# Head norms: each tile's sum of squares issued inside the next tile's products, and a gate chunk ahead of the first attention

## What is computed

```python
q = rmsnorm(q.reshape(bsz, s, B_HEADS, 2, B_HEAD_DIM), q_norm_g[l]).transpose(0, 2, 3, 1, 4)
k = rmsnorm(k.reshape(bsz, s, B_HEADS, 2, B_HEAD_DIM), k_norm_g[l]).transpose(0, 2, 3, 1, 4)
...
o = diff_attention(q, k, vb, lam, slopes)
...
gates = jax.nn.sigmoid(h @ w_gate[l] + b_gate[l])
```

## Time and profile before

| | |
|---|---|
| Median of 3 runs | 1939.25 us (1938.33 to 1940.53) |
| Profiled execution, its own time | 1938.46 us |
| Its span | 1936.5 us |
| Granted TensorE clock, mean | 0.965 |
| Busy: TensorE, its weight loads | 1814.7 us, 1333.3 us |
| Busy: VectorE, GpSimd, ScalarE | 898.5 us, 719.3 us, 590.1 us |

### The profile page before, as it was taken

One profiled execution on the slowest core, in us unless ns is written; L12 is line 12 of the kernel. 1 busy time (PEld: TensorE's weight loads), 2 busy tenths in 40 slices (PEclk: granted clock), 3 DMA queues, 4 the chain that ended last, 5 costly groups with the idle time before them and its releaser, 6 DMA issues.

```text
span 1936.5 us, 22752 instructions
## 1 busy us (share of the span) xinstructions
PE 1814.7 (94%) x8562; PEld 1333.3 (69%) x8562; DVE 898.5 (46%) x1267; ACT 590.1 (30%) x1085; POOL 719.3 (37%) x413
## 2 busy tenths in 40 slices
PE   5999979999998899999799889999989979999999
PEld 3888757775876444443488776777767868888887
DVE  4220665654453233332523576999438663303331
ACT  2323334444233111010232334555335222212221
POOL 4444323333340100000121447888814424444442
PEclk8999989999998899999889899999999989999999
DMA  5322222224343699999422332112253313332221
GB/s 198 98 77 98 78 75 66 82 82 141 95 133 120 237 396 394 343 365 375 170 77 86 132 97 92 68 66 71 77 195 108 121 56 108 98 98 90 96 97 44
DMA packets 81892, 266.32 MB, mean 138 GB/s; under 512 B 8320, under 2 KB 9344, under 8 KB 81792
## 3 DMA queue, kind: packets, MB, share of 16 engines
q1 hardware_dynamic: 60864, 222.32, 32.4%
q10 hardware_dynamic: 18624, 34.21, 5.0%
q0 software_dynamic: 2304, 8.39, 1.3%
HBM read 248.11 MB, written 16.78 MB: 137 GB/s over the span
## 4 chain that ended last, share of the span: by engine, by line
PE 86%; DVE 7%; DMA 3%; ACT 2%; issue 1%; ACTq 1%; POOL 0%; SPq 0%; DVEq 0%
PE psum L550 83%; DMA more<-stream 2%; DVE root L1769 1%; PE psum L1147 1%; DVE area_r L1743 1%; PE psum L846 1%; ACTq L1680 1%; PE psum L641 1%; DVE area L2273 1%; DVE root L1748 1%; ACT root L1290 1%; ACT area L1290 1%; PE psum L808 0%; DMA area<-xT 0%; DVE area L1750 0%
## 5 line engine op out<-in xcount | busy, mean ns | idle before, releaser
L550 PE MATMUL psum<-area_r,ring_hi 128*128 128x512 f32 (+1 forms) x3168 | 1001.0, 398 | 18.2 <-DVE area_r L1743 11.7
L451 POOL TENSOR_TENSOR ring_lo<-ring,ring_hi 128x1024 fp32r<-128x1024 f32 x220 | 534.3, 2432 | 980.4 <-ACT ring_hi L1290 980.4
L550 PEld LDWEIGHTS psum<-area_r,ring_hi 128*128 128x128 f32 x3168 | 595.2, 191 | 162.6 <-issue 27.9
L550 PE MATMUL psum<-area_r,ring_lo 128*128 128x512 f32 (+1 forms) x1584 | 621.3, 392 | 0.0
L1290 ACT ACTIVATE ring_hi<-ring 128x1024 fp32r<-128x1024 f32 x220 | 231.8, 1057 | 624.2 <-PE psum L550 595.7
L550 PEld LDWEIGHTS psum<-area_r,ring_lo 128*128 128x128 f32 x1584 | 301.8, 191 | 63.3
L1290 ACT ACTIVATE area<-psum 128x512 f32<-128x512 f32 (+3 forms) x257 | 124.9, 512 | 192.9 <-PE psum L641 71.4
L1769 DVE RECIPROCAL root<-root 128x512 f32<-128x512 f32 (+1 forms) x30 | 94.1, 3137 | 135.6 <-ACT root L1290 135.6
L550 PE MATMUL psum<-area 128*64 128x128 f32 (+6 forms) x832 | 112.1, 346 | 15.9 <-DVE area L1770 9.7
L550 PE MATMUL psum<-ring_hi,area_r 128*128 128x512 f32 (+1 forms) x352 | 107.2, 385 | 15.7 <-DVE area_r L1743 15.5
L1743 DVE TENSOR_TENSOR area_r<-area,area_r 128x512 fp32r<-128x512 f32 (+1 forms) x90 | 115.1, 1278 | 3.1
(11 more groups left out here) (211 smaller groups left out, 1594.9 us busy)
## 6 DMA issues: line engine op xcount, KB each, us to landing
ring<-stream SPq DMA_DIRECT2D x324, 512.0 KB, 3.6
more<-stream SPq DMA_DIRECT2D x48, 1024.0 KB, 8.4
area<-gates ACTq DMA_DIRECT2D x40, 256.0 KB, 6.2
gates<-root ACTq DMA_DIRECT2D x24, 256.0 KB, 2.0
gates<-area ACTq DMA_DIRECT2D x16, 256.0 KB, 3.5
area<-xT SPq DMA_DIRECT2D x8, 256.0 KB, 7.9
area<-xT ACTq DMA_DIRECT2D x8, 256.0 KB, 3.3
tokens<-area ACTq DMA_DIRECT2D x2, 1024.0 KB, 4.2
```

The lines of the kernel that those rows point to most:

```text
L451: nc.gpsimd.tensor_tensor(ring_lo[:, c % RS, :], ring[:, c % R, :], ring_hi[:, c % RS, :].bitcast(F32), ALU.subtract).then_inc(w_lo, 1)
L550: return nc.tensor.matmul(out, lhsT, rhs, start=first, stop=last)
```

## The change

TensorE's sum of tile j - 1 stands after the fourth of the eight steps of tile j, the last tile's sum behind it. For "qk" a `tail` puts two steps of gate chunk 0 before that last sum and the other six after it. `gate1` then starts at unit 2. ScalarE takes the root of tile j - 1 first, then the square of tile j, and rounds the next chunk after it; it copies gate chunk 0 out ahead of the attention. VectorE, GpSimd and SyncE are not edited.

```diff
--- before.py
+++ after.py
@@ -586,26 +586,37 @@
                                       k == 0, k == KD - 1)
                     ins.then_inc(weights_used, 1)
 
-            def normed(name, entries, lag=2, prior=None):
+            def normed(name, entries, prior=None, tail=None):
 
                 n_e, b0 = len(entries), HB[name]
-                for j in range(n_e + lag):
-                    if j < n_e:
-                        c, base, n, _, _, _, _ = entries[j]
-                        if j >= 4:
-                            pe.wait_ge(S("hdout"), b0 + j - 3)
-                        elif prior is not None:
-                            prior(j)
-                        by_tile(c, j % 4, rhs_of(base), n)
-                    if j >= lag:
-                        jj = j - lag
-                        n, mat = entries[jj][2], entries[jj][5]
-                        pe.wait_ge(S("hdsq"), b0 + jj + 1)
-                        if jj >= 2:
-                            pe.wait_ge(S("hdroot"), b0 + jj - 1)
-                        mm(psum[:, 4 + jj % 2, 0:n], mat[:], area[:, (SCR if name == "qk" else SCR2) + jj % 2, 0:n],
-                           True, True).then_inc(
-                            S("hdsum"), 1)
+
+                def squares(j):
+
+                    n, mat = entries[j][2], entries[j][5]
+                    pe.wait_ge(S("hdsq"), b0 + j + 1)
+                    if j >= 2:
+                        pe.wait_ge(S("hdroot"), b0 + j - 1)
+                    mm(psum[:, 4 + j % 2, 0:n], mat[:], area[:, (SCR if name == "qk" else SCR2) + j % 2, 0:n],
+                       True, True).then_inc(S("hdsum"), 1)
+
+                for j in range(n_e):
+                    c, base, n, _, _, _, _ = entries[j]
+                    if j >= 4:
+                        pe.wait_ge(S("hdout"), b0 + j - 3)
+                    elif prior is not None:
+                        prior(j)
+                    wait_chunk(c)
+                    rhs = rhs_of(base)
+                    for k in range(KD):
+                        if k == KD // 2 and j:
+                            squares(j - 1)
+                        ins = mm3(psum[:, j % 4, 0:n], parts(c, P * k, P * k + P), rhs(k), k == 0, k == KD - 1)
+                    ins.then_inc(weights_used, 1)
+                if tail is not None:
+                    tail(0)
+                squares(n_e - 1)
+                if tail is not None:
+                    tail(1)
 
             def attention(kind, fill=None):
                 units, maps = score_items(kind)
@@ -695,23 +706,27 @@
                 token_major(C0["vb"] + 4 * hf, 4 * hf, tokens(HH1, HL1), NT, lambda k: None)
 
             pe.wait_ge(S("v_out"), 12)
-            normed("qk", qk_entries())
-            pe.wait_ge(S("hdout"), HB["qk"] + 16)
-            pe.wait_ge(consts, 21 + HEADS1)
             def gate1(u):
 
                 n, half = divmod(u, 2)
+                gate1_steps(n, range(4 * half, 4 * half + 4))
+
+            def gate1_steps(n, ks):
+
                 c = C0["gate1"] + n
-                if half == 0:
+                if 0 in ks:
                     wait_chunk(c)
                     if n:
                         pe.wait_ge(S("gate_raw"), n)
-                for k in range(4 * half, 4 * half + 4):
+                for k in ks:
                     ins = mm3(psum[:, 7, :], parts(c, P * k, P * k + P), (tr(HH1 + k), tr(HL1 + k)), k == 0, k == KD - 1)
-                if half:
+                if KD - 1 in ks:
                     ins.then_inc(weights_used, 1)
 
-            attention("diff", fill=gate1)
+            normed("qk", qk_entries(), tail=lambda x: gate1_steps(0, range(2, KD) if x else range(2)))
+            pe.wait_ge(S("hdout"), HB["qk"] + 16)
+            pe.wait_ge(consts, 21 + HEADS1)
+            attention("diff", fill=lambda u: gate1(u) if u >= 2 else None)
 
             def spread(lo, hi):
 
@@ -1317,24 +1332,24 @@
                 A(root[:, 0, 0:n], psum[:, bank, 0:n], ACT.Sqrt, bias=eps[:, 0:1], scale=1.0 / D).then_inc(
                     S("normroot"), 1)
 
-            def normed(name, entries, lag=1):
+            def normed(name, entries):
 
                 b0 = HB[name]
-                for j in range(len(entries) + lag):
-                    if j < len(entries):
-                        c, _, n, _, _, _, _ = entries[j]
-                        follow(c + 1)
-                        if j >= 2:
-                            act.wait_ge(S("hdsum"), b0 + j - 1)
-                        A(tile((SCR if name == "qk" else SCR2) + j % 2, n), psum[:, j % 4, 0:n], ACT.Square).then_inc(S("hdsq"), 1)
-                    if j >= lag:
-                        jj = j - lag
+                for j in range(len(entries) + 1):
+                    if j:
+                        jj = j - 1
                         n, inv = entries[jj][2], entries[jj][6]
                         act.wait_ge(S("hdsum"), b0 + jj + 1)
                         if jj >= 2:
                             act.wait_ge(S("hdout"), b0 + jj - 1)
                         A(root[:, jj % 2, 0:n], psum[:, 4 + jj % 2, 0:n], ACT.Sqrt, bias=eps[:, 0:1],
                           scale=inv).then_inc(S("hdroot"), 1)
+                    if j < len(entries):
+                        c, _, n, _, _, _, _ = entries[j]
+                        act.wait_ge(weights_used, c + 1)
+                        A(tile((SCR if name == "qk" else SCR2) + j % 2, n), psum[:, j % 4, 0:n], ACT.Square).then_inc(
+                            S("hdsq"), 1)
+                        follow(c + 1)
 
             def attention(kind, fill=None):
                 units, maps = score_items(kind)
@@ -1399,7 +1414,7 @@
             A(lamt[:, 2:4], lamt[:, 0:2], ACT.Exp).then_inc(S("lam_e"), 1)
             def gate1(u):
 
-                if u % 2 == 0 and 2 <= u <= 4 * KD:
+                if u % 2 == 0 and 4 <= u <= 4 * KD:
                     n = u // 2 - 1
                     act.wait_ge(weights_used, C0["gate1"] + n + 1)
                     if n >= 2:
@@ -1411,6 +1426,9 @@
                     act.wait_ge(S("gate_raw"), n + 1)
                     act.dma_start(gates_dram[n], tile(STAGE1 + n % 2)).then_inc(S(f"gate_kept{n % 2}"), 16)
 
+            act.wait_ge(weights_used, C0["gate1"] + 1)
+            A(tile(STAGE1), psum[:, 7, :], ACT.Copy).then_inc(S("gate_raw"), 1)
+            follow(C0["gate1"] + 1)
             attention("diff", fill=gate1)
 
             act.wait_ge(S("do"), 4 * HEADS1)
```

## The result

| | before | changed |
|---|---|---|
| Median of the runs made side by side | 1938.79 us (4 runs, 1935.95 to 1940.53) | 1926.27 us (4 runs, 1923.43 to 1927.93) |
| Ratio, 95% interval | | 0.9928 (0.9916 to 0.9941) |
| Profiled execution: span | 1936.5 us | 1925.9 us |
| TensorE busy; mean clock | 1814.7 us; 0.965 | 1814.8 us; 0.967 |

The kernel is faster by 12.5 us by the medians and 14.0 by the ratio (0.0072 x 1939.25, 11.4 to 16.3 by its interval), where 9.9 was forecast. By the ratio the changed kernel takes 1925.3 us (1923.0 to 1927.9 by the interval), just under the forecast's lower end of 1925.5. When it was run again among the experiments its ratio was 0.9937 (0.9918 to 0.9955), 12.2 us. So the direction and most of the size came out, and the gain was forecast about 3 us too small.

The account below looks back on a forecast made before the run. TensorE was taken as the bound, busy 1814.7 of 1936.5 us. 1938.46 - 13.3 (first attention) + 3.4 (q2 and km) = 1928.6 us on the profile's scale, 1929.4 as a median; range 1925.5 to 1934.5.

Parts of the forecast that it names:

- Steps 1 to 4: q and k stage to attention unit 2: moved sums and gate chunk cut TensorE's 9.7 us wait to 1.0, gaining 13.3 us.
- Steps 1 and 2: q and k stage: two more sums ahead of the last product (1.83 us later) and mid-tile sums with 1.9 us slack cost nothing.
- kv: The two-tile kv stage: TensorE waits about 0.8 us for the second Square, as before; change taken as 0.
- Step 5: q2's first sum: TensorE asks for it earlier and waits for the memory tiles' norm, a new wait of 3.7 us.
- Step 7: q2: GpSimd's instruction holds VectorE's conv tap, which ends at +4.8 us after a tile instead of +2.9.
- Step 8: Memory keys (km) behind q2: TensorE waits 3.2 us instead of 2.93; without clock losses the new order is 1.8 us late.
- E: End of q2's last product, forecast at 1138.38 us instead of 1132.86.
- Step 9: Clock at q2 and km: 1.6 us lost behind the first wait, 1.5 behind km's, as today; total loss there 3.4 us.
- A: Rival: q2 is milder, the tap goes first, km's wait shrinks to 1.3 us, clock may stay up; 1926.0 us, chance 0.20.
- B: Rival: clock takes more, two slow stretches each at q2's and km's waits, one at the attention; 1934.5 us, chance 0.15.
- C: Rival: sums inside a tile's products drag TensorE's clock down in q, k and q2; over 1943 us possible, chance 0.05.
- D: Rival: the fill brings nothing, as unit 2 waits for unit 0's softmax; 2.5 us returns, 1931.9 us, chance 0.10.

Follow-up runs that it names:

- both: Changed kernel with q2's first two sums later and km's squares not waiting for all of q2's outputs: 1919.77 us, ratio 0.99 (0.9884 to 0.9916).
- all three: Changed kernel with q2's first two sums later, km's squares not held by q2's outputs, and conv taps behind km's norms: 1915.15 us, ratio 0.9891.

## Why the prediction was off, point by point

- **Steps 1 to 4, the first layer.** Forecast 13.3 us, measured 13.44 in the stage, with the wait 0.83 for 1.0. Steps 1 and 2 are right: the period stayed at 6.35 us, with no wait inside. The prediction gave no split; it is 7.15 for the fill and 6.26 for the sums.
- **kv.** Taken as 0. TensorE's wait for the second Square is 0.69 us in the changed kernel and 0.77 before, so this holds; the stage itself varies by more than it could show.
- **Step 5.** Forecast a wait of 3.7 us, measured 3.51 to 3.56. Taking the wait away by a later sum took 3.8 us off the stage although another stretch of half clock came.
- **Step 7.** Forecast: the tap ends 1.9 us later. It took 2.40 us instead of 0.74, 1.7 more, and without taps the wait at km was 1.95 us shorter. The rule of the Trainium skill, "SBUF — State Buffer", section "Who interferes with whom", gave here what the rows of the old order in this stage could not show, and the trace agrees with it.
- **Step 8.** Forecast a wait of 3.2 us, measured 3.01. Then 0.47 and not 0.6 ahead of the last sum. The terms of step 8 add up to E + 18.95 and not 19.1, which changes nothing. Without clock losses on either side the new order is 1.5 us late, where 1.8 was forecast: 87.67 less 1.6 for its one fall, against 84.56. So these sizes account for 0.3 us.
- **Step 9 is the term that failed.** I charged 1.6 us of clock behind the first wait and 1.5 behind km's. The charge was by the length of the wait, and the length does not decide. The first fall came (3.4 us at half clock). The second did not: in none of the five traces of the changed order with this stage unedited did the clock fall behind the 3.01 us; once it did, in the trace with the later first sum. That is why the stage lost 1.6 us and not 3.4. And I had nothing for the part behind km, where the old order lost 1.6 us to a fall ahead of its attention in five of six traces (the fill alone, and the old order in the second layer, counted with it) and the changed order in none of five. The two make 1.8 + 1.6 = 3.4 us, nearly all that lies between the forecast's 9.9 and what the stages add up to, 13.4 - 1.6 + 1.6 = 13.4; measured were 12.2 to 14.0.
- **What stays open.** Whether that missing fall is owed to the order or to luck. It is not luck alone. Two traces of the changed order in which q2 began 2.03 and 2.04 us after the clock's last return to 1.00 had neither fall, and five of the old order, with 1.88 to 2.12 us, had both. The old order had neither when q2 began at 1.58 us (its third trace). Nor is it a mark of the new order as such: of its six edited forms, five had the fall behind the scores' 2.21 us again (taps later, km's squares early, both, all three, between tiles), and the other had the one behind 3.01 us. So it seems to hang on when a wait comes in relation to the clock's last change, and the changed kernel has its waits, not by design, where the clock stayed up. No run changed that moment alone, so this is read from the traces and not shown by experiment.
- **Rivals.** A (milder q2) was right in its time and wrong in its reason: the tap was held in every trace of the changed kernel, it was the clock that stayed up. B fell: the attention's start has a clock of 1.00, and q2 and km have one slow stretch between them. C fell with the period. D fell: unit 2's scores started 1.85 us after unit 0's, and its transpose came right behind its products.

## What to carry to other kernels

When an engine waits at a stage's end for a chain that ran in step with it, look first at how many links are queued there: one and a half tiles less lag saved nearly as much (6.3 us) as 24 products put into the wait (7.2), and the two add up. A tighter order must be checked where the stage starts too: a lag that is slack at the end is cover at the start, and q2 lost 3.55 us there until its first two sums were put later. Cut traces into stages before explaining a difference of a few us. Here a stage that the change never touches took 461.6 or 464.0 us in one and the same kernel, and single traces of either kernel would have told a false story.

## What the runs showed of the hardware

- The clock's falls are not fixed by a wait's length. Behind 2.93 us of waiting in the same kernel at the same place it fell in two of three traces (0.52 in the window behind it in the first) and stayed at 1.00 in the third; behind 3.01 us in the changed order it stayed up in five traces and fell in one that differs only ahead of it. Behind the same 2.21 us ahead of the scores it fell in ten of 17 traces, and it also fell behind 2.48 and 1.94 us (sums between tiles).
- At the waits of 3.5 us or more ahead of the first attention and at q2's first sum it fell each time: for 3.4 us at 3.55 and 3.56 us (6.8 us once, at 3.51), for 6.8 to 13.7 us at 4.95 to 9.71 us, counted from the fall, which lay partly within these waits.
- A wait of 0.8 us ahead of an attention's first scores left it at 1.00.
- A VectorE instruction with two inputs in SBUF that starts while GpSimd's runs is held until that one ends: taps that came 0.39, 0.54 and 0.91 us behind its start took 2.53, 2.38 and 2.01 us instead of 0.74, and all ended 0.55 us behind the end of GpSimd's (2.38 us). In q2 it came so for six tiles on end, five of them at the same distance; the reciprocal and the output beside it kept their 3.35 and 0.75 us. It works the other way too: q2's first tap came 0.2 us ahead of GpSimd's instruction and took 0.74, and GpSimd's took 2.78.
- A f32 sum between fp32r products costs 0.91 us wherever in the group of products it stands.
